# Mixture-of-experts stage: experts taken in order of their row counts, the four smallest multiplied unsplit in full fp32 on two column halves of the array

## The reference, cut to what matters

```python
logits = xt @ router_w                                  # 256 tokens x 8 experts
top_vals, top_idx = lax.top_k(logits, 2)
gates = one_hot(top_idx) * softmax(top_vals)            # summed over the two choices
for e in range(8):                                      # w13[e]: 1024 x 7168, w2[e]: 3584 x 1024
    out = out + gates[:, e:e + 1] * ((silu(xt @ w13_gate[e]) * (xt @ w13_up[e])) @ w2[e])
```

## Time and profile before

| | |
|---|---|
| median of 3 runs (lowest, highest) | 1497.52 us (1497.34, 1497.89) |
| span of the profiled execution | 1495.6 us |
| TensorE busy | 1480.1 us, 99% |
| VectorE, ScalarE busy | 1189.5 us (80%), 976.1 us (65%) |
| loaded and stored by DMA | 463.75 MB, mean 310 GB/s |
| the eight items on TensorE | 533.3 us to 1483.5 us |

### The profile page before, as it was taken

One profiled execution on the slowest core, in us unless ns is written; L12 is line 12 of the kernel. 1 busy time (PEld: TensorE's weight loads), 2 busy tenths in 40 slices (PEclk: granted clock), 3 DMA queues, 4 the chain that ended last, 5 costly groups with the idle time before them and its releaser, 6 DMA issues.

```text
span 1495.6 us, 21517 instructions
## 1 busy us (share of the span) xinstructions
PE 1480.1 (99%) x7443; PEld 1242.1 (83%) x7443; DVE 1189.5 (80%) x1070; ACT 976.1 (65%) x934; POOL 40.3 (3%) x51
## 2 busy tenths in 40 slices
PE   9999999999999999999999999999999999999997
PEld 7989888887989878888888888888888888888885
DVE  6676754447477689888888888888889889988888
ACT  6445543345445567777777777777777777777775
POOL 2000000000000010000000000000000000001000
PEclk9999999999999999999999999999999999999999
DMA  8737655535435369999999999999999999999993
GB/s 313 293 141 297 243 195 202 188 141 184 170 113 212 113 244 423 378 388 383 368 389 380 379 373 390 380 369 397 372 373 400 371 378 388 373 377 388 421 394 122
DMA packets 69179, 463.75 MB, mean 310 GB/s; under 512 B 7629, under 2 KB 9053, under 8 KB 16264
## 3 DMA queue, kind: packets, MB, share of 16 engines
q1 hardware_dynamic: 61976, 437.22, 76.0%
q0 software_dynamic: 7152, 25.86, 4.6%
HBM read 455.84 MB, written 15.60 MB: 315 GB/s over the span
## 4 chain that ended last, share of the span: by engine, by line
PE 95%; DVE 3%; issue 1%; ACT 1%; DVEq 0%; ACTq 0%
PE bank L1386 29%; PE bank L1388 29%; PE bank L1387 29%; PE bank L1781 2%; DVE w_lo L825 1%; PE bank L1474 1%; PE bank L1428 1%; PE bank L1595 0%; PE bank L1770 0%; PE bank L1515 0%; PE bank L1578 0%; PE bank L1525 0%; PE bank L1513 0%; PE bank L1654 0%; DVE xn L865 0%
## 5 line engine op out<-in xcount | busy, mean ns | idle before, releaser
L831 DVE TENSOR_TENSOR w_lo<-raw,w_hi 128x2048 fp32r<-128x2048 f32 x333 | 762.8, 2292 | 98.8 <-ACT w_hi L507 96.4
L507 ACT ACTIVATE w_hi<-raw 128x2048 fp32r<-128x2048 f32 x333 | 638.2, 1916 | 125.0 <-PE bank L1388 124.5
L1386 PE MATMUL bank<-w_hi,yT_hi 128*128 128x512 f32 x1528 | 602.9, 395 | 2.1 <-DVE yT_lo L837 0.8
L1388 PE MATMUL bank<-w_hi,yT_lo 128*128 128x512 f32 x1528 | 595.8, 390 | 0.0
L1387 PE MATMUL bank<-w_lo,yT_hi 128*128 128x512 f32 x1528 | 594.9, 389 | 0.0
L1386 PEld LDWEIGHTS bank<-w_hi,yT_hi 128*128 128x128 f32 x1528 | 287.0, 188 | 62.2 <-DVE yT_lo L837 1.7
L1388 PEld LDWEIGHTS bank<-w_hi,yT_lo 128*128 128x128 f32 x1528 | 286.8, 188 | 60.7
L1387 PEld LDWEIGHTS bank<-w_lo,yT_hi 128*128 128x128 f32 x1528 | 287.2, 188 | 57.2
L825 DVE TENSOR_TENSOR w_lo<-raw,w_hi 128x1024 fp32r<-128x1024 f32 x160 | 188.2, 1220 | 42.2 <-ACT w_hi L501 40.9
L501 ACT ACTIVATE w_hi<-raw 128x1024 fp32r<-128x1024 f32 x160 | 160.4, 1055 | 40.3 <-PE bank L1388 40.3
L837 DVE TENSOR_TENSOR yT_lo<-bank,yT_hi 128x512 fp32r<-128x512 f32 (+1 forms) x96 | 61.5, 656 | 50.7 <-ACT yT_hi L559 45.2
(11 more groups left out here) (255 smaller groups left out, 947.2 us busy)
## 6 DMA issues: line engine op xcount, KB each, us to landing
raw<-in_moe_units SPq DMA_DIRECT2D x336, 1024.0 KB, 7.4
raw<-in_layer_units SPq DMA_DIRECT2D x44, 1024.0 KB, 4.9
raw<-in_dense_units SPq DMA_DIRECT2D x33, 1024.0 KB, 5.6
sent<-in_x POOLq DMA_DIRECT2D x1, 6144.0 KB, 34.6
xn<-sent POOLq DMA_DIRECT2D x8, 512.0 KB, 8.4
done<-qk POOLq DMA_DIRECT2D x7, 512.0 KB, 9.1
done<-in_x POOLq DMA_DIRECT2D x1, 2048.0 KB, 40.7
x<-in_x SPq DMA_DIRECT2D x2, 512.0 KB, 4.1
```

The lines of the kernel that those rows point to most:

```text
L507: act.activation(w_hi[:, st.split(u), :, :].rearrange("p a n -> p (a n)"), raw[:, st.slot(u), :], ACT.Copy)\
L831: dve.tensor_tensor(w_lo[:, st.split(u), :, :].rearrange("p a n -> p (a n)"), raw[:, st.slot(u), :], w_hi[:, st.split(u), :, :].rearrange( ...
L1386: pe.matmul(out, hi_l, hi_r, start=start, stop=False, skip_group_check=True)
L1388: return pe.matmul(out, lo_l, hi_r, start=False, stop=stop, skip_group_check=True)
```

## The change

Experts 1 to 7 are ranked by their counts (expert 0 stays first). The four smallest, ranks 0 to 3, become **few items** of at most 64 rows, the items 1, 3, 5 and 7; the three others stay full items of 128 row places at 2, 4 and 6. An expert above its cap (64 or 128) gets an additional item at the end; up to four are provided for.

A few item is not split. TensorE reads the fp32 block straight out of `raw`; the 64 rows are the stationary operand, and the block's columns are dealt out to the two column halves of the array, whose results land in partitions 0 to 63 and 64 to 127 of one bank. An up or gate block is 8 matmuls of 256 columns, a down block 4 of 512. The last of them frees the slot. ScalarE and VectorE have only silu, gating and copies to do. The slots get a semaphore each (`free0` to `free5`) in place of `raw_free`.

```diff
-OVER = 3
+OVER = 4
+FEW = 64
+PAIRED = 3
...
         def load(st, u, src, width=UNIT):
-            hold(sp, "raw_free", st.upto(u))
+            hold(sp, f"free{st.slot(u)}", st.freed(u))
...
-                               io["x"][0].unsqueeze(1).broadcast_to([T, (OVER + 1) * P // T, D]))\
+                               io["x"][0].unsqueeze(1).broadcast_to([T, ITEMS * P // T, D]))\
                     .then_inc(sem("done_filled"), 16)
...
-        with act.Fori(1, NE) as i:
-            item(i)
+        with act.Fori(0, PAIRED) as p:
+            few_item(p * 2 + 1, p)
+            item(p * 2 + 2, p + 1)
+        few_item(NE - 1, PAIRED)
+        few_rows_out(NE - 1, last_y)
...
-                if first and j == 2:
+                if first and j == 1:
+                    experts_by_count()
+                elif first and j == 2:
+                    places()
+                elif first and j == 3:
                     gates()
-                if first and j == 3:
+                elif first and j == 4:
                     last_rows()
...
+            def few_up(u, between, b):
+
+                for m in range(2):
+                    if m == 1 and between is not None:
+                        between()
+                    slot = st.slot(u + m)
+                    pe.wait_ge(sem(f"raw{slot}"), st.landed(u + m))
+                    for k in range(4):
+                        for col in range(2):
+                            a = k * 512 + col * 256
+                            mm = pe.matmul(bank[b][col * FEW:(col + 1) * FEW, 0:256], few_x[:, 4 * m + k, :],
+                                           raw[:, slot, a:a + 256], start=(m == 0 and k == 0), stop=(m == 1 and k == 3),
+                                           skip_group_check=True)
+                            if k == 0 and col == 0:
+                                mm.then_inc(sem("unit_used"), 2)
+                    mm.then_inc(sem(f"free{slot}"), 2)
...
+            def few_down(u, j, m):
+                slot = st.slot(u)
+                pe.wait_ge(sem(f"raw{slot}"), st.landed(u))
+                for half in range(2):
+                    for col in range(2):
+                        a = half * 1024 + col * 512
+                        mm = pe.matmul(bank[4][col * FEW:(col + 1) * FEW, :], few_hT[j % 2][:, half, m * FEW:(m + 1) * FEW],
+                                       raw[:, slot, a:a + 512], start=(j == 0 and m == 0 and half == 0),
+                                       stop=(j == ITEM_STEPS - 1 and m == 1 and half == 1), skip_group_check=True)
...
+        item(0, 0, turn_few_rows, first=True)
+        with pe.Fori(0, PAIRED) as p:
+            few_item(p * 2 + 1, p, turn_rows)
+            item(p * 2 + 2, p + 1, turn_few_rows)
+        few_item(NE - 1, PAIRED)
```

More of the change, by code:

```diff
@@ L262, in _build @@
     pick = sb("pick", [P, OVER, NE])
-    first = sb("first", [P, OVER + 2])
+    first = sb("first", [P, 1 + OVER + NE])
     last_s = sb("last_s", [P, 4, NT])
@@ L282, in _build @@
     number = pool_u[:, 0, 128:128 + OVER * NE].rearrange("p (k e) -> p k e", k=OVER)
+    fewer, level_e = above[:, 0, :, :], level[:, 0, :, :]
+    counted, rank_e, is_few, cap, place_e, is_last, total = (sizes[:, n, :] for n in range(7))
+    last_pos, last_one, last_two = (last_at[:, n, :] for n in range(3))
+    n_over = last_s[:, 0, 0:1]
     place8 = pool_b[:, 1, 0:NT * NE].rearrange("p (t e) -> p t e", t=NT)
@@ L917, in hidT_lo @@
                 rest(yT_lo[s], banks4(g_bank + t)[:, 0:n, :], yT_hi[s]).then_inc(sem("hidT_lo"), 1)
-        dve.sem_inc(sem("raw_free"), 2 * RAW)
+        for slot in range(RAW):
+            dve.sem_inc(sem(f"free{slot}"), 2)
         dve.memset(eps_col[:, :], EPS).then_inc(sem("consts"), 1)
@@ L1279, in _ @@
-        c.wait()
-        c.step(dve.tensor_reduce(row[:, :, :], row8, AX.X, ALU.add))
-        dve.tensor_copy(info[0:1, :], first[0:1, :]).then_inc(sem("info_ready"), 1)
-        c.wait()
-        dve.tensor_copy(row_i[:, :, :], row[:, :, :]).then_inc(sem("rows_known"), 1)
-        lo(layer_stream(DEPTH - 1), 24)
+        c.step(dve.tensor_copy(total, bank[3][:, 0:NE]))
+        gathered_lo(0)
+        lo(layer_stream(DEPTH - 1), 23)
+        lo(layer_stream(DEPTH - 1), 24)
+        square8 = [P, NE, NE]
@@ L1342, in item, with few_item @@
             lo_whole(st, ITEM_UNITS - 1)
-        item(0, first=True)
+        def few_item(i):
+            for j in range(ITEM_STEPS):
+                dve.wait_ge(sem("silu"), i * ITEM_STEPS + (j + 1) + NT * DENSE_TURNS)
+                dve.tensor_tensor(hid[:, 0, 0:2 * P], hid[:, 0, 0:2 * P], bank[j % 2][:, 0:2 * P], ALU.mult)\
+                    .then_inc(sem("hid_ready"), 1)
+        item(0, 0, first=True)
+        with dve.Fori(0, PAIRED) as p:
+            few_item(p * 2 + 1)
+            item(p * 2 + 2, p + 1)
+        few_item(NE - 1)
         dve.wait_ge(sem("info_ready"), 1)
         n_items = dve.value_load(info[0:1, 0:1], min_val=NE, max_val=ITEMS)
-        with dve.Fori(1, NE) as i:
-            item(i)
         with dve.If(n_items > NE):
-            item(NE)
+            item(NE, PAIRED + 1)
             with dve.If(n_items > NE + 1):
-                item(NE + 1)
+                item(NE + 1, PAIRED + 2)
                 with dve.If(n_items > NE + 2):
-                    item(NE + 2)
+                    item(NE + 2, PAIRED + 3)
+                    with dve.If(n_items > NE + 3):
+                        item(NE + 3, PAIRED + 4)
+                    dve.nop()
                 dve.nop()
@@ L1771, in turn_rows, with turn_few_rows, item @@
                 mm.then_inc(sem("gather_mm"), 1)
+        def turn_few_rows(i):
+            hold(pe, "xg_in", i * 16)
+            for b in range(2):
+                for k in range(4 * b, 4 * b + 4):
+                    mm = pe.transpose(bank[6][:, k * FEW:(k + 1) * FEW], xg[0:FEW, k * P:(k + 1) * P], ident[0:FEW, 0:FEW])
+                mm.then_inc(sem("gather_mm"), 1)
         gs = (xgT_hi, xgT_lo)
-        def item(i):
+        def item(i, o, then=None, first=False, over=False):
             st = item_stream(i)
```

347 lines of the change are left out of this document (231 added, 116 removed).

## The result

The changed kernel takes 1463.91 us (median of 4 runs, 1462.85 to 1465.76); the kernel before, beside it on the same chip, 1497.43 us (4 runs, 1497.31 to 1497.89). The ratio is 0.9778, with a 95% interval from 0.9764 to 0.9792. It is faster, by 33.5 us where 59.7 were forecast: inside the range, but only a little more than half of the gain came. The profiled execution's own time is 1465.76 us, its span 1463.9, so the forecast's -60 stands against a change of the span of -31.7.

What follows compares the result with a forecast made beforehand. TensorE bounds at 2.82 us a block, with loads behind at 2.48. Items sum 125.1 + 3 x 97.1 + 95.9 + 3 x 123.6 + 3 x 2.8 = 891.5 against 950.2; with the end about -60, so 1438 us, range 1408 to 1480.

Steps and rivals of the forecast that it cites:

- A few block on TensorE: Few items' matmuls: both column halves work at once, 1.73 us an up block, 1.76 a down block.
- The loads as the new bound: Few items: loads at 422 GB/s, 2.48 us a block, bound them instead of TensorE.
- The third rival: Loads do not hold 422 GB/s: at some 360, 2.9 us a block bounds items 1 to 7; 1525 us, chance 0.03.
- The few items: Items 1, 3, 5: 94.6 us at the loads' pace plus 2.5 for POOL's store and fetch, 97.1 us each.
- The last few item: Item 7: as the other few items but fetching nothing for a following item, 95.9 us.
- The wait of a full item: Start of items 2, 4, 6: TensorE waits about 5.1 us for the first block's landing and split.
- The clock behind it: Full items after that wait may begin at half clock: one block at double length, 2.8 us for each of three.
- Item 0: First full item: gets the ranking chains that stood ahead of it, 4.5 us more, 125.1 us.
- The first fetch: Fetch of rows ahead of item 1: moves from 576.5 to about 620 us, lands by 630, 17 us of cover left.
- The end: After the last block: four last matmuls on alternate row halves may pair, copy is one later operation; net 1 us less.
- The second rival: Clock falls inside the few items: some 112 us each, four times 15 more, 1497 us; chance 0.05.
- The range: Whole kernel: 1408 to 1480 us, from the forecast's own bounds of 28 less and 38 plus 8 more.

Runs made afterwards that it cites:

- idle matmuls: Changed kernel plus 18 matmuls on old data, results unread, behind each of the three few items ahead of a full one: 1460.46 us, ratio 0.9748.
- the last one: Changed kernel with pairs unrolled on TensorE, first part of ranking chain ahead of item 0, jump ahead of last few item, 18 unused matmuls per border: 1452.16 us, ratio 0.9699.
- halves: Changed kernel with a full item's first block split in two halves, so TensorE can begin after half of it: 1465.36 us, ratio 0.9779.

## Why the prediction was right, and which terms were mis-sized

**A few block on TensorE** (1.73 to 1.76 us, between bounds of 1.73 and 3.5): right. Opposite corners of 64 x 64 foretold two column halves over all 128 rows: 0.105 us apart in the changed kernel, 0.107 with nothing to wait for, 0.217 on one half.

**The loads as the new bound, 2.48 us a block at 422 GB/s**: right, shown from both sides. Half the matmuls saved 3.6 us, half the bytes 104. One of the signs named for it, that VectorE's busy time would halve, came only in part: it fell from 1189.5 to 781.1 us of the whole span. The third rival falls with it: 422 to 423 GB/s stood for tens of us at a time. The limit of about 358 GB/s that the Trainium skill, "DMA: Bandwidth & Descriptors", section "Where 436 GB/s comes from", states didn't bind here.

**The few items** (97.1): 99.3, 98.4 and 99.9, each some 2 us more. The forecast let 36 of 42 blocks run at 422 from the item's start. The windows show where that fails: 353 GB/s from 662 to 675 us, 340 from 890 to 905, 279 from 1116 to 1130, and then 419 to 423 to each item's end. Behind the two pauses the full slots hold the loads back, as shown above. Ahead of item 1 there is no pause, and the DMA engines are busy (0.93) but move less; POOL's fetch and store of rows run there. What each part of this 2 us is worth was not tried, and the forecast's count of POOL's bytes one for one is shown for the last few item alone.

**The last few item** (95.9, "fetches nothing"): 104.9. This step of the prediction failed. The item holds four gathers of earlier results, 2 MB, which the kernel before had there too, hidden behind a TensorE bound. The prediction asked what the change moves, not what was already standing under a cover that the change takes away. Without them it took 99.5; of the other 3.6 us some 2 are those of every few item, and 1.5 stayed open.

**The wait of a full item** (5.1 us): 4.99, 4.96, 4.96. **The clock behind it** (2.8 us each): half clock came, with 4.0 to 6.0 us of each stretch over matmuls, at the first border 14 of them where 12 were taken, but its price was 0.4 to 1.3 us, since the landings of the first blocks stand right behind. A full item and its clock together had 121.3 us; 121.6, 120.6 and 121.0 were measured between pauses.

**Item 0** (125.1, with 4.5 for the chains): 128.2. The chain's length was right, 558.37 to 562.95 us or 4.6 on VectorE, where 4.7 was worked out. What was missed is that a TensorE wait of 3.7 us in the middle of an item also brings half clock, a thing that the prediction saw only at the borders: 5.2 us of work at half clock, so some 2.6 us. Moving the chain returned 5.1 us of the item. The first fetch stood at 625.5 us, where 620 was forecast, and made nothing wait.

**The end** ("net 1 us less"): 5.5 more than that. The matmuls ran in the 1.99 us forecast, but jumping over the code that isn't taken costs 4.6 us, and the jump at the end of each round of the loop 2.4. In the sum these pauses had no term at all. Alone, taking them away gave 5.5 and 5.1 us.

**The second rival** (clock falls inside the few items) had next to no share in the missing gain. In the changed kernel gaps of some 0.5 us left the clock at 1.00 (window 675 to 700); the one fall inside a few item is 3.4 us long, from 1117.2, behind the pause of 2.33. With half the matmuls the mean clock was 0.74, and the time was no worse. The Trainium skill, "TensorE: Matmul & The Clock Gate", section "HAM oscillation — how this bites in real kernels", tells of a kernel of few rows that waits some 3 to 5 us for its data ahead of every group of matmuls and falls to half clock each time. The changed kernel's waits for loads inside few items are 1.83 us at most, so it is no such case; but with half the matmuls the clock fell at 704.1 us though the waits around it were 1.4 us at most, so a fall doesn't need waits of 3 us. It falls inside the last few item, near 1355 us, in three of the variants too (idle matmuls, unrolled loop, the last one), around waits of 2.0 to 2.6 us for a load.

**The range** was worked out from 1436, the forecast less the 1.9 us between span and median: from 1438 its own terms give 1410 to 1484 and not 1408 to 1482. The result lies inside by either.

The terms sum up: about 9 us for the last few item, 6 for the other three, 9 for pauses at the jumps, 3 for item 0's chain. Orders in which the few items stand together, with one border instead of three, and a ring of more than six slots were not tried.

## What to carry to other kernels

When a change moves the bound from compute to loads, list every other transfer in the stage, also those that the change doesn't touch: each now costs its bytes over the bandwidth. Price an alternating schedule by its borders, and look there first for what a shorter wait uncovers: two attempts to shorten the border (idle matmuls, halves) returned about 1 us a border and nothing, because a landing stood right behind it. In a stretch that the loads bound, a pause of TensorE is lost as soon as the slots are full. Narrow full-fp32 matmuls on two column halves run in pairs, so they take half the time that they take on one half (0.105 against 0.217 us a record).

## What the runs showed of the hardware

- Pauses of 1.0 to 3.3 us on TensorE with nothing to wait for stand at a loop's jump back, behind code that is jumped over, and at the first code behind it. They go when the loop is unrolled or the skipped code is absent, and move when the code is moved (3.12 us ahead of the last few item). Packets of the queue "q8 instruction" start where they begin, within 0.5 us for the four of the changed kernel, and are absent there where the pause is gone, so that they are a fetch of instructions is borne out by the traces. The packets' number by itself says little: 66 against 31 before, but 62 with the loop unrolled and 64 without the skipped code. The kernel before had one such pause of 0.61 us at its end.
- The same jump at the end left no pause where TensorE had some 6 us of matmuls to do when the first of these packets started (one column half, 1613.2 to 1619.1 us).
- Waits of 3.7 to 5.0 us each came with a stretch of 3.4 or 6.8 us at the 1.2 GHz level, which began during the wait or within 1.6 us of its end. Behind shorter ones it came in some cases: not at the pause of 2.40 us ahead of item 3, for 3.4 us at the one of 2.33 ahead of item 5.
- Four matmuls that lie in the two row halves of the array in turn took 1.99 us where four over 128 rows took 3.67. The column halves pair likewise, and for them a run on one half shows it.
